# Mixture-of-experts groups of 64 rows as groups of 32, transposed on VectorE, in a two-layer encoder

## What is computed

```python
def swiglu(t, w_gate, w_up, w_down):
    return (jax.nn.silu(t @ w_gate) * (t @ w_up)) @ w_down
...
    for e in range(N_EXPERTS):
        out = out + combine[:, e:e + 1].astype(t.dtype) * swiglu(t, w_gate[e], w_up[e], w_down[e])
```

## Time and profile before

| what | us |
|---|---|
| median of 3 runs | 1340.64 |
| lowest and highest | 1339.22 and 1342.0 |
| the profiled execution, its own time | 1340.69 |
| span of its profile | 1339.0 |
| TensorE busy in that span | 1287.6 |

### The profile page before, as it was taken

The page is one execution under the profiler, slowest core; times in us unless marked ns, Lnnn a source line. Parts: engine busy times, 40 slices in busy tenths (PEclk is TensorE's granted clock), DMA queues, the critical chain, the costliest instruction groups (busy, mean ns, idle before and its releaser), DMA issues.

```text
span 1339.0 us, 20505 instructions
## 1 busy us (share of the span) xinstructions
PE 1287.6 (96%) x8949; PEld 804.7 (60%) x8949; DVE 554.4 (41%) x806; ACT 441.6 (33%) x660; POOL 10.8 (1%) x35
## 2 busy tenths in 40 slices
PE   7999999998998999999799999999999999999997
PEld 6787788877787665768657476633333354333343
DVE  5585555546586574644757465310000001200003
ACT  6564444436553463533536355200000000000001
POOL 3000000000000000000000000000000000000000
PEclk9999999999998999999999999999999999999999
DMA  9235544264004999999999999999999999999991
GB/s 351 108 135 206 216 186 183 89 241 172 18 0 190 419 420 402 420 365 414 404 394 384 402 421 417 417 420 420 419 384 359 360 357 355 388 377 407 418 415 57
DMA packets 129067, 418.75 MB, mean 313 GB/s; under 512 B 4248, under 2 KB 8384, under 8 KB 128976
## 3 DMA queue, kind: packets, MB, share of 16 engines
q1 hardware_dynamic: 127872, 416.30, 78.9%
q0 software_dynamic: 544, 1.12, 0.3%
q10 hardware_dynamic: 560, 0.01, 0.0%
HBM read 416.37 MB, written 1.05 MB: 312 GB/s over the span
## 4 chain that ended last, share of the span: by engine, by line
PE 87%; DVE 5%; ACT 3%; DMA 3%; issue 1%; ACTq 0%; SPq 0%; DVEq 0%
PE bank L2066 27%; PE bank L2137 14%; PE bank L1705 14%; PE bank L1706 13%; PE bank L1707 13%; DMA ring<-in_moe_w_down 3%; PE bank L2002 2%; PE bank L1996 2%; PE bank L2085 1%; ACT raw_d L782 1%; DVE lo L1090 1%; DVE mx L1180 1%; DVE raw_d L1177 1%; DVE w_lo L1524 1%; ACT hi L716 1%
## 5 line engine op out<-in xcount | busy, mean ns | idle before, releaser
L1524 DVE TENSOR_TENSOR w_lo<-ring,w_hi 128x1024 fp32r<-128x1024 f32 x168 | 201.9, 1224 | 62.7 <-ACT w_hi L716 55.1
L2066 PE MATMUL bank<-ring,late_acts 128*32 128x256 f32 (+3 forms) x1936 | 215.8, 434 | 0.0
L716 ACT ACTIVATE w_hi<-ring 128x1024 fp32r<-128x1024 f32 x168 | 174.9, 1059 | 93.2 <-PE bank L1707 77.4
L1705 PE MATMUL bank<-hi,act_hi 128*128 128x512 f32 (+1 forms) x400 | 157.0, 392 | 10.3 <-DVE lo L1090 6.6
L2066 PEld LDWEIGHTS bank<-ring,late_acts 128*32 128x32 f32 (+1 forms) x1936 | 85.7, 120 | 121.5 <-issue 100.8
L2137 PE MATMUL bank<-ring,at_buf 128*32 128x256 f32 (+1 forms) x1408 | 157.1, 450 | 0.5 <-ACT at_buf L716 0.5
L716 ACT ACTIVATE at_buf<-bank 128x256 f32<-128x256 f32 (+2 forms) x40 | 18.0, 449 | 414.4 <-PE bank L2085 414.4
L1707 PE MATMUL bank<-hi,act_lo 128*128 128x512 f32 (+1 forms) x400 | 153.9, 385 | 0.0
L1706 PE MATMUL bank<-lo,act_hi 128*128 128x512 f32 (+1 forms) x400 | 153.9, 385 | 0.0
L1546 DVE TENSOR_TENSOR silu_buf<-silu_buf,bank 128x512 f32<-128x512 f32 (+2 forms) x56 | 29.4, 536 | 227.5 <-PE bank L2066 194.1
L1090 DVE TENSOR_TENSOR lo<-raw_gu,hi 128x1024 fp32r<-128x1024 f32 x96 | 112.3, 1221 | 24.4 <-ACT hi L716 23.6
(11 more groups left out here) (240 smaller groups left out, 1255.5 us busy)
## 6 DMA issues: line engine op xcount, KB each, us to landing
ring<-in_moe_w_up SPq DMA_DIRECT2D x50, 2048.0 KB, 14.3
ring<-in_moe_w_down SPq DMA_DIRECT2D x49, 2048.0 KB, 13.6
ring<-in_moe_w_gate SPq DMA_DIRECT2D x48, 2048.0 KB, 13.0
raw_gu<-in_w_in SPq DMA_DIRECT2D x7, 2048.0 KB, 12.3
ring_after<-in_moe_w_gate SPq DMA_DIRECT2D x7, 2048.0 KB, 9.7
ring_after<-in_moe_w_down SPq DMA_DIRECT2D x7, 2048.0 KB, 12.0
ring_after<-in_moe_w_up SPq DMA_DIRECT2D x6, 2048.0 KB, 14.3
raw_gu<-in_dense_w_gate SPq DMA_DIRECT2D x5, 2048.0 KB, 7.9
```

What stands on the lines that cost most here:

```text
L716: return nc.scalar.activation(out, in_, ACT.Copy, **kw)
L1524: v.tensor_tensor(w_lo[:, n % WP, :], flat(u)[:, q * 1024:(q + 1) * 1024], w_hi[:, n % WP, :], ALU.subtract).then_inc(w_lo_done, 1)
L1705: mm(out, ah, wh, start=start, stop=False, **kw)
L2066: ins = mm(bank[b][c * g.n:(c + 1) * g.n, 0:width], acts[STEPS[s][0]][:, k, g.col:g.col + g.n], by_rows(u, n)[:, kl, c * width:(c + 1) * w ...
```

## The change

Six things are changed, all in the experts' part.

1. Groups of 64 become groups of 32: capacity 96 has three, 64 has two. Where a group's sums stand in PSUM and its rows in `yt` now come from two tables, `SUM_OF` and `ROW_OF`.
2. A small group's result is no longer transposed by TensorE and copied by ScalarE. VectorE transposes it in 32x32 squares from `silu_buf` to `at_buf` (or `at_late`, or the room of `first_acts0`). For that the gate and up products take their weight columns in another order: for each quarter of the array runs of 32 columns at a distance of 128.
3. In a unit that has wide and small groups the small ones now come first, and for down too.
4. `load` waits for a wide unit's slot until its remainders are made and its small groups are through, no longer until the wide products are through.
5. The rows of `yt` are laid out so that pair 0 and pair 1, and pair 2 and pair 3, share tile 1. So pairs 1 and 3 have only four `rows` extras in front of them, and pairs 0 and 2 only one table transpose.
6. `rows_out` of pair 0's large expert stands behind the four remainders of pair 1's first unit on VectorE; at the end of the kernel the copies of the last pair are spread over ScalarE and VectorE group by group.

Its diff, cut to what matters here:

```diff
+ROW_OF = {(0, 0, 0): (0, 0), (0, 0, 1): (0, 64), (0, 0, 2): (1, 32), (0, 1, 0): (1, 0),
...
+SUM_OF = {(0, 0, 0): (3, 0), (0, 0, 1): (4, 0), (0, 0, 2): (6, 0), (0, 1, 0): (6, 256),
...
-        if self.full:
-            self.gate = i
-            self.up = i if fulls == 2 else 1
-            self.acc = (3, 4)[i] if w == 0 else (6 if other >= 128 and other % 64 == 0 else 4)
...
+        self.j = i if self.wide or w == 1 or first == 0 else i - 2
+        self.n = 64 if self.wide else 32
+        self.first_slot = self.n * i if self.wide or w == 1 else first + 32 * self.j
+        self.col = (CAPS[PAIRS[p][0]] - first if w else 0) + 32 * self.j
+        if self.wide:
+            self.gate = self.up = i
+        elif w == 0 and first > 0:
+            self.gate = self.up = 5
         else:
-            self.gate = 5
-            self.up = 5 if fulls else 0
-            self.acc = 6
-            self.acc_col = 256 * w if shared_sums(p) else 0
-        self.tile, self.row = w, 64 * i
-        if w == 0 and i == 2:
-            self.tile, self.row = 1, CAPS[PAIRS[p][1]]
-
-
-GROUPS = {(p, w): [Group(p, w, i) for i in range((CAPS[PAIRS[p][w]] + 63) // 64)] for p in range(NP) for w in range(2)}
+            self.gate = (0, 5, 1)[i]
+            self.up = self.gate if cap > 32 else 1
+        self.acc, self.acc_col = SUM_OF[p, w, i]
...
 def extra_kind(p, n):
 
     if n < 8:
+        if p % 2 == 1:
+            return ("rows", 0, n - 4) if n >= 4 else None
         return ("rows", n // 4, n % 4) if p > 0 else None
-    if n in (8, 9):
+    if n == 8 or (n == 9 and p % 2 == 1):
         return ("gates", n - 8, 0)
     if n >= 12 and n % 3 == 0 and p < NP - 1:
         return ("gather", (n - 12) // 3, 0)
...
             def load(u, dst, src):
 
-                if BEFORE[u] >= 0:
-                    sp.wait_ge(unit_used, BEFORE[u] + 1)
+                b = BEFORE[u]
+                if b in FIRST_PIECE:
+                    sp.wait_ge(w_lo_done, FIRST_PIECE[b] + 4)
+                if b >= 0 and (UNIT_READ[b] or SLOT[u] != SLOT[b]):
+                    sp.wait_ge(unit_used, b + 1)
+                if b >= 0 and UNIT_READ[b] and SLOT[u] != SLOT[b]:
+                    sp.wait_ge(w_used, PIECE_USES[FIRST_PIECE[b] + 3])
...
                 def rows_out(p, w):
                     for g in GROUPS[p, w]:
                         if g.wide:
-                            c = g.buf
-                            ins = v.tensor_copy(yt[0:WIDE, 0, c * 512:(c + 1) * 512], bank[g.acc][:, :])
+                            ins = v.tensor_copy(yt[0:WIDE, 0, g.j * 512:(g.j + 1) * 512], bank[g.acc][:, :])
                             continue
-                        m = 2 if g.full else 4
-                        width = D // m
-                        for c in range(1 if (p, w) == (NP - 1, 1) else m):
-                            ins = v.tensor_copy(yt[g.row:g.row + g.n, g.tile, c * width:(c + 1) * width],
-                                                bank[g.acc][c * g.n:(c + 1) * g.n, g.acc_col:g.acc_col + width])
+                        if (p, w, g.j) == (NP - 1, 1, 1):
+                            dve.wait_ge(unit_used, N_UNITS)
+                        for c in range(2 if p == NP - 1 else 4):
+                            ins = v.tensor_copy(yt[g.row:g.row + 32, g.tile, c * 256:(c + 1) * 256],
+                                                bank[g.acc][32 * c:32 * c + 32, g.acc_col:g.acc_col + 256])
...
-                        v.tensor_tensor(e_silu[g.buf][:, 0:n], e_silu[g.buf][:, 0:n], bank[g.up][:, 0:n],
-                                        ALU.mult).then_inc(e_gated_done, 1)
+                        gated_e = e_silu(s, g)[:, 0:n]
+                        v.tensor_tensor(gated_e, gated_e, bank[g.up][:, 0:n], ALU.mult).then_inc(e_gated_done, 1)
+                    n = BLOCKS[STEPS[s][2]][1] // 4
+                    if len(small_groups(s)) > 0:
+                        dve.wait_ge(e_gated_done, SUMS[s + 1])
+                    for g in small_groups(s):
+                        v.transpose(e_at(s, g)[:, 0:n], e_silu(s, g)[:, 0:n]).then_inc(small_at_done, 1)
 
...
                             if u == 1:
                                 build_sel(1)
+                            if i == 0 and p > 0 and u == FIRST_UNIT["g", s]:
+                                rows_out(p - 1, 0)
                         extra(p, 3 * i)
...
-                    if s > 0 and STEPS[s - 1][2] == NB - 1:
-                        dve.wait_ge(unit_used, last_unit("d", s - 1) + 1)
+                    if s > 0 and STEPS[s - 1][2] == NB - 1 and not (s < NS - 1 and wide(s - 1) and wide(s + 1)):
+                        u = last_unit("d", s - 1)
+                        if s == NS:
+                            dve.wait_ge(first_sum_done, 1)
+                        else:
+                            dve.wait_ge(unit_used, u + 1)
+                        if wide(s - 1) and UNIT_READ[u]:
+                            dve.wait_ge(w_used, PIECE_USES[FIRST_PIECE[u] + 3])
                         rows_out(*STEPS[s - 1][0:2])
...
                     if kind == "rows":
-                        pe.wait_ge(y_out, 2 * (p - 1) + a + 1)
+                        pe.wait_ge(y_out, 2 * p if p % 2 == 1 or a == 1 else 2 * p - 1)
...
                 def products(s, what, i, n):
 
                     u = FIRST_UNIT[what, s] + i
-                    if wide(s):
-                        wide_products(s, what, i, n)
-                    else:
-                        landed(u)
                     kk = UCOLS // n
                     small = small_groups(s)
+                    if len(small) > 0:
+                        landed(u)
+                    if u < 2:
+                        pe.wait_ge(first_lo, 2 * u + 2)
                     for g in small:
                         if what == "u" and i == 0 and g.up == g.gate:
                             pe.wait_ge(e_silu_done, summed(s, groups_of(s).index(g)))
-                        b, m = g.gate if what == "g" else g.up, 128 // g.n
-                        width = n // m
+                        b = g.gate if what == "g" else g.up
                         for kl in range(kk):
                             k = i * kk + kl
-                            for c in range(m):
-                                ins = mm(bank[b][c * g.n:(c + 1) * g.n, 0:width],
-                                         acts[STEPS[s][0]][:, k, g.col:g.col + g.n],
-                                         by_rows(u, n)[:, kl, c * width:(c + 1) * width],
-                                         start=k == 0, stop=k == KT - 1)
+                            w = by_rows(u, n)[:, kl, :].rearrange("p (t a j) -> p a t j", a=4, j=32)
+                            for c in range(4):
+                                ins = mm(bank[b][32 * c:32 * c + 32, 0:n // 4], acts[STEPS[s][0]][:, k, g.col:g.col + 32],
+                                         w[:, c], start=k == 0, stop=k == KT - 1)
                         if g is small[-1]:
                             ins.then_inc(unit_used, 1)
                         elif i == n // 512 - 1:
                             ins.then_inc(gate_done if what == "g" else up_done, 1)
+                    if wide(s):
+                        wide_products(s, what, i, n)
...
-                    if b == 0 and w == 0 and shared_sums(p):
-                        mm(bank[6][:, :], zeros[:, 0:P], zeros[:, :], start=True, stop=True)
+                    if b == 0 and w == 0:
+                        for z in joint_banks(p):
+                            mm(bank[z][:, :], zeros[:, 0:P], zeros[:, :], start=True, stop=True)
                     small = small_groups(s)
...
+                        for g in small:
+                            own = g.acc not in joint_banks(p)
+                            for tl in range(4):
+                                f = 4 * i + tl
+                                for c in range(4):
+                                    ins = mm(bank[g.acc][32 * c:32 * c + 32, g.acc_col:g.acc_col + 256],
+                                             e_at(s, g)[:, 32 * f:32 * f + 32],
+                                             by_rows(u, D)[:, tl, c * 256:(c + 1) * 256],
+                                             start=own and b == 0 and f == 0, stop=b == NB - 1 and f == n // P - 1,
+                                             skip_group_check=not own)
+                            if s == NS - 1 and g is small[0]:
...
-                    turns = len(groups_of(s - 1)) if s > 0 else 0
+                    turns = len(wide_groups(s - 1)) if s > 0 else 0
                     if s > 0:
                         pe.wait_ge(e_gated_done, SUMS[s])
+                    if turns > 0:
                         turn(s - 1, 0)
                     if i == 0 and p > 0:
                         pe.wait_ge(extra_out, EXTRA[p - 1, 21])
                     products(s, "g", 0, n)
-                    if turns > 1:
+                    if turns > 0:
```

(8 more changed lines are left out.)

159 lines of the change are left out of this document (79 added, 80 removed), and 10 rows, old and new, of tables (ROW_OF, SUM_OF).

## The result

| kernel | median us | against before, 95% interval |
|---|---|---|
| before | 1341.32 (4 runs) | |
| changed | 1318.06 (4 runs, 1316.59 to 1320.28) | 0.983, 0.981 to 0.985 |

The change makes the kernel 23 us faster. I had forecast 50 us, and the time lies 4 us above the upper end of my range. The profiled execution of the changed kernel took 1320.28 us, its span is 1318.5.

The account below looks back on a forecast made before the run. TensorE's own stream was taken as the bound. Forms 15.1, transposes 18.8, dropped rows and table transposes 9.2 and pair 0's order 10 make 53 us; 1340.7 - 53 + 2 (DMA take-back) = 1290 us, range 1277 to 1314.

Parts of the forecast that it names:

- a floor worked out from bandwidth: Pairs 0 and 1: at 5.07 us a unit the 83rd lands no earlier than 842 us, allowing about 19 us gain.

Follow-up runs that it names:

- e6: The changed kernel with each 256-column gate and up matmul in pair 2's second block (1024 wide) cut into two of 128; 1338.97 us.
- e7: e6 with every weight transfer into a slot that held a unit before bringing only a quarter of it; 1301.25 us.

## What to carry to other kernels

Where an edit cuts matmuls into smaller ones, work out how long a packet of instructions lasts in the shortest of them, and compare it with the distance of the instruction queue's packets where the DMA is full; the average over the kernel hides it, the block with the fewest columns decides. Runs of a round number of records between waits for "issue" are the mark of it.

When small work is put ahead of large work on one engine, put what it depends on ahead on the other engines as well. And a floor worked out from bandwidth must start from the transfers as they are, with their pauses for slots, and end not where data land but where they can be used.

## What I had not expected of the hardware

- TensorE's instructions come through the same DMA as data, in packets of 16 KB, 256 instructions of 64 bytes. With all of the weights' traffic (382 GB/s over e6's starved stretch, 348 over the changed kernel's) most packets follow the one before by 5.9 to 6.2 us when TensorE starves. At a quarter of the traffic the closest come 3.5 us apart, the pace at which TensorE takes them.
- Fed fast enough (e7), TensorE does float32 matmuls of 32x128 on a quarter of the array at 27 ns a record (192 in 5.26 us), and twice as many records for the same columns cost 0.08 us a unit (5.26 against 5.18). Whether still shorter ones would hit a floor was not tried.
- VectorE transposes 128x256 float32 in squares of 32 in 0.37 us, and pieces of 32x64 from one quarter of the partitions to another in 0.19 us.
